# YOCO-style decoder trunk on one core: eight filler products instead of 24 at each of the three stage entries

## What is computed

```python
for l in range(DEPTH):                      # DEPTH = 2
    shift, scale, gate = ada_mod(c_act, mod_mix_w[l], mod_mix_b[l], 3)
    if l == N_A_LAYERS:
        k_sh, v_sh = shared_kv(x, ...)      # norm, modulation, k and v products
    h = rms_norm(x, norm_pre_mix[l]) * (1.0 + scale) + shift
    y = dilated_mixer(h, ...) if l < N_A_LAYERS else diff_mixer(h, k_sh, v_sh, ...)
    x = x + gate * rms_norm(y, norm_post_mix[l])
    shift, scale, gate = ada_mod(c_act, mod_ffn_w[l], mod_ffn_b[l], 3)
    h = rms_norm(x, norm_pre_ffn[l]) * (1.0 + scale) + shift
    y = conv_ffn(h, ...)                    # gate and up products, conv, gelu, down product
    x = x + gate * rms_norm(y, norm_post_ffn[l])
```

## Time and profile before

| what | value |
|---|---|
| median of 3 runs | 1460.94 us |
| lowest and highest | 1459.55 and 1462.33 us |
| the profiled execution, its own time | 1459.9 us |
| its span, first to last instruction | 1458.0 us |
| mean granted TensorE clock over the span | 0.986 |
| PE busy | 1407.2 us (97%) |
| DVE busy | 889.1 us (61%) |
| ACT busy | 588.7 us (40%) |

### The profile page before, as it was taken

The page is one execution under the profiler, slowest core; times in us unless marked ns, Lnnn a source line. Parts: engine busy times, 40 slices in busy tenths (PEclk is TensorE's granted clock), DMA queues, the critical chain, the costliest instruction groups (busy, mean ns, idle before and its releaser), DMA issues.

```text
span 1458.0 us, 18234 instructions
## 1 busy us (share of the span) xinstructions
PE 1407.2 (97%) x7091; PEld 1153.7 (79%) x7096; DVE 889.1 (61%) x1572; ACT 588.7 (40%) x1018; POOL 146.2 (10%) x250
## 2 busy tenths in 40 slices
PE   4999999999999999999999999998999999999998
PEld 3789888888798788887887787776888878887886
DVE  7777877674458777763556538887358444443223
ACT  4533444345443334332124526776443333332212
POOL 2001100000211111110112101221221000000000
PEclk9999999999999999999999999998999999999999
DMA  9437423331146655552661221212126333232321
GB/s 334 140 85 233 145 88 117 101 102 30 29 137 199 185 169 178 179 182 87 202 188 58 87 73 58 59 59 87 30 85 186 92 96 92 88 100 89 100 89 70
DMA packets 168667, 171.51 MB, mean 118 GB/s; under 512 B 5269, under 2 KB 140806, under 8 KB 168582
## 3 DMA queue, kind: packets, MB, share of 16 engines
q1 hardware_dynamic: 154224, 119.59, 27.2%
q0 software_dynamic: 13824, 50.34, 10.7%
q10 hardware_dynamic: 534, 0.41, 0.1%
HBM read 168.22 MB, written 2.10 MB: 117 GB/s over the span
## 4 chain that ended last, share of the span: by engine, by line
PE 82%; DVE 8%; ACT 4%; issue 3%; POOL 2%; DMA 1%; SPq 0%; ACTq 0%; DVEq 0%; POOLq 0%
PE ps L624 19%; PE ps L552 15%; PE ps L554 15%; PE ps L553 15%; PE ps L1087 3%; PE ps L900 2%; PE ps L793 2%; PE ps L864 2%; ACT prob L1702 2%; PE ps L606 1%; PE ps L595 1%; PE ps L1204 1%; DVE prob L2355 1%; POOL osum L2537 1%; PE ps L674 1%
## 5 line engine op out<-in xcount | busy, mean ns | idle before, releaser
L552 PE MATMUL ps<-hhi,whi 128*128 128x512 f32 (+1 forms) x1008 | 398.6, 395 | 5.2 <-DVE hlo L1890 4.6
L1815 DVE TENSOR_TENSOR wlo<-raw,whi 128x1024 fp32r<-128x1024 f32 x200 | 244.0, 1221 | 245.7 <-ACT whi L1312 245.4
L554 PE MATMUL ps<-hhi,wlo 128*128 128x512 f32 (+1 forms) x1008 | 390.5, 387 | 0.0
L553 PE MATMUL ps<-hlo,whi 128*128 128x512 f32 (+1 forms) x1008 | 390.1, 387 | 0.0
L1312 ACT ACTIVATE whi<-raw 128x1024 fp32r<-128x1024 f32 x200 | 210.1, 1052 | 257.1 <-PE ps L624 175.7
L552 PEld LDWEIGHTS ps<-hhi,whi 128*128 128x128 f32 x1008 | 191.4, 190 | 47.0 <-issue 6.4
L554 PEld LDWEIGHTS ps<-hhi,wlo 128*128 128x128 f32 x1008 | 191.4, 190 | 41.9
L553 PEld LDWEIGHTS ps<-hlo,whi 128*128 128x128 f32 x1008 | 191.7, 190 | 39.6 <-issue 1.0
L1940 DVE SCALAR_TENSOR_TENSOR macc<-mraw,csil,macc 128x256 f32<-128x256 f32 x294 | 142.2, 484 | 13.4 <-DMA mraw<-in_mod_ffn_w_dram 4.2
L624 PE MATMUL ps<-whi,ghi 128*128 128x512 f32 x352 | 110.8, 396 | 1.7 <-DVE tmp L2294 1.7
L624 PE MATMUL ps<-whi,glo 128*128 128x512 f32 x352 | 110.8, 396 | 0.0
(11 more groups left out here) (282 smaller groups left out, 2031.1 us busy)
## 6 DMA issues: line engine op xcount, KB each, us to landing
mraw<-in_mod_ffn_w_dram POOLq DMA_DIRECT2D x48, 512.0 KB, 4.2
raw<-in_ffn_w_gate_dram SPq DMA_DIRECT2D x44, 512.0 KB, 3.8
raw<-in_ffn_w_up_dram SPq DMA_DIRECT2D x44, 512.0 KB, 3.8
raw<-in_ffn_w_down_dram SPq DMA_DIRECT2D x44, 512.0 KB, 3.6
mraw<-in_mod_mix_w_dram POOLq DMA_DIRECT2D x32, 512.0 KB, 3.9
raw<-in_a_w_qkv_dram SPq DMA_DIRECT2D x28, 512.0 KB, 4.1
mstart<-in_mod_mix_w_dram SPq DMA_DIRECT2D x8, 1024.0 KB, 14.5
mraw<-in_kv_mod_w_dram POOLq DMA_DIRECT2D x16, 512.0 KB, 3.8
```

The lines of the kernel that those rows point to most:

```text
L552: pe.matmul(out_, whi[:, slot, cols], rhs_hi, start=first, stop=False)
L553: pe.matmul(out_, whi[:, slot, cols], rhs_lo, start=False, stop=False)
L554: return pe.matmul(out_, wlo[:, slot, cols], rhs_hi, start=False, stop=last)
L1815: dve.tensor_tensor(wlo[:, slot, :], raw[:, slot, :], head, ALU.subtract).then_inc(*at.here(lo_ready, ahead))
```

## The change

The constant WARM goes from 24 to 8. It is used at the three entries and nowhere else.

```diff
-    WARM, WARM_START, WARM_SUMS = 24, 8, 12
+    WARM, WARM_START, WARM_SUMS = 8, 8, 12
```

## The result

| | before | after |
|---|---|---|
| median of 20 runs | 1460.24 us | 1462.64 us |
| lowest | 1457.54 us | 1460.4 us |
| span of the profiled execution | 1458.0 us | 1460.3 us |
| mean granted TensorE clock | 0.986 | 0.981 |

The ratio after to before is 1.0020, with a 95% interval of 1.0012 to 1.0028: slower by 1.8 to 4.1 us. The medians differ by 2.40 us. The effect is small, but the interval excludes zero; it sits right at the line of 0.2% that the prediction drew. (One of the 20 runs of before took 2085 us; the ratio leaves it out.)

What follows compares the result with a forecast made beforehand. PE was taken to bound the kernel, busy for 1407.2 of 1458.0 us. Terms of 0.6, 0.1 and 1.7 us at the three entries sum to +2.4 us on the median of 1460.94, giving 1463.3 us; range 1461.0 to 1466.0 us.

Steps and rivals of the forecast that it cites:

- The direct gain of 0: At the three entries: removing 16 fillers only lengthens PE's wait for DVE, so the first product stays; 0 us.
- each microsecond lost at entry 1 is one at the end: Behind the first groups: PE and the DVE chain have no slack, so losses at entries 1 and 3 reach the end.
- entry 1: First group of 24 products at entry 1: the low clock takes in its start too; +0.6 us, bounds 0 and +0.74.
- entry 2: First group of 12 products at entry 2: almost nothing was fast before; +0.1 us, bounds 0 and +0.7.
- The term of entry 3: First group at entry 3, where the clock held before: it now falls; +1.7 us, bounds +1.47 and +2.21.
- The bound of 0.74: Upper bound at entry 1: all 24 products at the lower level, 0.214 us each, 5.14 against 4.40 us.
- The clock falls at all three entries, and now inside the idle time: Before the first products: idle times of 6.21, 6.08 and 5.19 us mean the first product already finds the clock low.
- The pattern low, low, held: Before the change: clock low in the first groups of entries 1 and 2 (0.62), held at entry 3 (1.00).
- That eight do as well as 24, or 24 as badly as eight: Rival at the entries: before falls at all three, or after holds at one; 0 to +1 us, 1461.4 us; chance 0.17.
- That the clock stays low through the turns: Rival at the 32 turn matmuls behind each first group: up to 3.5 us lost per entry, 1469.8 us; chance 0.11.
- That some of the turns run low: Rival: whole first groups and a few turns run low; +3.6 up to +4.5 us, about 1464.6 us; chance 0.26.
- That the filler slows ACT beside it: ACT's roundings beside the filler, 2.14 against 2.01 us: less contention shortens the seams by 0 to -0.4 us; chance 0.02.
- a sign that a low clock can outlive dense work: Stretch from 1004 to 1014 us: low for 10 us while PE was busy for 7.44; cited for the third rival.

Runs made afterwards that it cites:

- filled waits: 36, 35 and 31 fillers at entries 1, 2 and 3, as many as fit in the wait, against the kernel before with 24: ratio 0.9982, -2.6 us.

## Why the prediction was right

**The result stands where it was put**: 1462.64 us against 1463.3 us, a difference of medians of 2.40 us against a sum of 2.4. That the two agree to the last digit is luck: the interval reaches from 1.8 to 4.1 us, and the trace's own sum is 2.76. The 0.7 us between 1462.64 and 1463.3 are in the median of before, which was 1460.94 over three runs and is 1460.24 over 20.

**The direct gain of 0** was right. The filler's end went away from the first product by 16 fillers, the waits grew by 3.45, 3.47 and 3.46 us (3.42 forecast), while the first product kept its distance from the second turn (9.99 us at entry 1 in both). DVE, ACT and POOL waited for none of it, and the run with 48 shows the other side: a filler that is not covered costs time. That each microsecond lost at entry 1 is one at the end fits too: from the turns of entry 1 to the second turn of entry 2 all eight traces take 385.9 to 386.1 us, and from the turns of entry 3 to the end 383.0 to 383.2, whatever the group in front of them took.

**The terms**, from the profiled execution of after: entry 1 +0.72 (forecast +0.6, upper bound 0.74), entry 2 +0.01 (+0.1), entry 3 +2.03 (+1.7, upper bound 2.21). The term of entry 3 was mis-sized by 0.3 us. The prediction priced it as half of a low stretch of before, "and a little for the earlier start"; in fact the whole wait for the clock falls behind the first product there, as at entry 1, and only the last products before 1077.31 us are fast. In this execution entries 1 and 3 lie near the upper bounds. The bound of 0.74 was itself too low, as the run with eight at entries 1 and 2 shows with 0.86 us: a low first product stands 0.35 us ahead of the second one, and the bound gave it 0.214. At entry 2 the extra low time at the front was given back at the end: the low products came first and the last four stood 0.23 us apart, in before the last three, so that the term came out at 0.01. The sum of the three, 2.76 us, lies between the measured 2.40 us of the medians and the 2.9 us of the ratio.

**"The clock falls at all three entries, and now inside the idle time"** was right in after, and in the runs without filler.

**The pattern low, low, held** was read from one execution. Two more executions show the same: in the run with eight at entry 3 alone, entries 1 and 2 (24 fillers) took 4.43 and 4.45 us; in the run with eight at entries 1 and 2, entry 3 (24 fillers) took 2.89 us. The Trainium skill's rule, that the low matmuls' number differs from run to run (TensorE: Matmul & The Clock Gate, "What's actually happening"), had been given as a reason that the pattern might be one draw. These three traces agree on the pattern, which is no proof that every execution has it. The traces do show draws of the kind that the rule means: entry 1 with eight fillers took 5.12 and 5.26 us in two executions, and the low stretch near 835 us is there in seven traces and missing in that of before.

**The rivals.** That eight do as well as 24, or 24 as badly as eight, was put at 0 to +1 us, and the interval starts at 1.8. The filled waits speak against it too: if the timed executions of before fell at entry 3 as well, they would have gained some 3.0 + 2.0 us, an estimate from the traces, and their interval ends at 4.1. That the clock stays low through the turns is ruled out by the turns' 1.00 in after, and without filler too. That some of the turns run low did not happen in after, where the group alone stayed low. It did happen in one trace at one entry, with eight fillers at entries 1 and 2, and cost 0.1 us there, so what the rival describes can occur, but no trace shows it at all three entries or at its price. That the filler slows ACT beside it falls as well: the pair of roundings that took 2.14 us beside the filler takes this long where the filler ended before it, here from the timeline of ACT in after, with the second half's pair:

```profile
394.80 2.14 ACT L1376 ACTIVATE hhi<-a_h 128x1024 fp32r<-128x1024 f32 x2
...
410.42 2.01 ACT L1376 ACTIVATE hhi<-a_h 128x1024 fp32r<-128x1024 f32 x2
```

**What was not seen.** The prediction looked at what the cut takes away and asked hardly what 24 fillers leave undone. The rows for it stood there: groups of 4.40 and 4.45 us at 0.62. The better change has the other sign, 36, 35 and 31 fillers, and gains 2.6 us (1.2 to 4.1).

## What to carry to other kernels

A filler has no worth by itself, only by the clock of the work behind it: read the granted clock and the duration of that first work before asking how long the filler should be. Here it kept the whole first group at full clock when it stopped 0.2 to 1.8 us short of the product that it serves. When it stopped some 2.7 us short it was worth little: 0.7 of the 2.2 us that a low clock costs at entry 1, and nothing at entry 2. Beyond the wait it costs about 0.18 us for each filler (7.58 / 42). Idle times between 1.8 and 2.7 us were not tried, so fewer fillers than 36 and 35 might do as well. A wait ended by a steady chain on other engines can be filled by count, as here, where the first product's distance from the second turn stayed the same to 0.1 us in every run but the one with 48. Where its length varies, the safe count would be that of the shortest wait; no run here shows such a case.

## What the runs showed of the hardware that I had not expected

- In these traces a longer idle time did not raise the price of a fall. After idle times from 5.23 to 7.97 us the first group took 4.9 to 5.3 us at entries 1 and 3, and 4.4 to 4.6 us at entry 2 (2.9 at full clock). The turns that follow had the full clock, but for the first 0.2 us or so of them in one execution (mean clock 0.97).
- With 24 fillers an idle time of 1.77 or 1.78 us left the first group at full clock, 2.66 to 2.79 us did not, in every trace that has it.
- A long low stretch at the end of layer 1's attention is there in each kernel's trace, with the filled waits too (granted clock 0.50 over 1002 to 1014 us there and in after). It starts and ends at slightly different places, in before at about 1004 us, and in the run with eight at entry 3 alone some 3 us of full clock stand in the middle of it (1.00 over 1006 to 1008 us). I had used it as a sign that a low clock can outlive dense work. At the entries it lasted at most about 5.5 us from the first product. What makes it last there was not tried.
